# Warm-up of the tensor engine ahead of the first token tile: turnings of the identity or products in four column groups

## The reference

```python
def rms_norm(x, gain):
    xf = x.astype(jnp.float32)
    y = xf * lax.rsqrt(jnp.mean(xf * xf, axis=-1, keepdims=True) + NORM_EPS)
    return (y * gain.astype(jnp.float32)).astype(x.dtype)

for layer in range(DEPTH):                 # DEPTH = 1
    xn = rms_norm(h, norm_mix_gain[layer])
    proj = xn @ w_in[layer]
    hq, hf_fwd, hf_bwd, hi, hg, aq, ak, av, gate_a, gate_b = jnp.split(proj, IN_SPLITS, axis=-1)
    y_rec = hgrn2_mixer(hq, hf_fwd, hf_bwd, hi, hg, lb_fwd_all[layer], lb_bwd_all[layer], hg_norm_gain[layer])
    y_att = window_attention(aq, ak, av, attn_sink[layer])
    merged = jax.nn.sigmoid(gate_a) * y_rec + jax.nn.sigmoid(gate_b) * y_att
    h = h + merged @ w_out[layer]
    h = h + moe_ffn(rms_norm(h, norm_ffn_gain[layer]), ...)   # 32 experts, 4 for each token
return rms_norm(h, final_norm_gain)
```

## Time and profile before

| | us |
|---|---|
| runs of the kernel | 1752.43, 1752.76, 1756.24 |
| their median | 1752.76 |
| span of the profiled execution, first to last instruction | 1751.3 |
| TensorE busy in it | 1724.3 (98%) |
| VectorE busy | 1441.9 (82%) |
| ScalarE busy | 1140.3 (65%) |
| GpSimd busy | 518.5 (30%) |

### The profile page before, as it was taken

One profiled execution on the slowest core, in us unless ns is written; L12 is line 12 of the kernel. 1 busy time (PEld: TensorE's weight loads), 2 busy tenths in 40 slices (PEclk: granted clock), 3 DMA queues, 4 the chain that ended last, 5 costly groups with the idle time before them and its releaser, 6 DMA issues.

```text
span 1751.3 us, 26655 instructions
## 1 busy us (share of the span) xinstructions
PE 1724.3 (98%) x8893; PEld 1275.0 (73%) x8893; DVE 1441.9 (82%) x1489; ACT 1140.3 (65%) x1126; POOL 518.5 (30%) x293
## 2 busy tenths in 40 slices
PE   8999999999999999999999999999999999999997
PEld 7778777777777867677777777777777777777765
DVE  4666676567655889999998999899989998999898
ACT  4544564455454577778777777777777777777783
POOL 1102201210220144223553354334423442344340
PEclk9999999999999999999999999999999999999998
DMA  7431333133125589999999999999999999999985
GB/s 212 145 97 56 88 108 96 48 108 96 48 97 224 189 342 390 352 350 402 382 386 380 370 370 375 382 367 372 377 381 370 368 381 380 368 365 384 381 329 232
DMA packets 159188, 488.19 MB, mean 279 GB/s; under 512 B 13250, under 2 KB 83186, under 8 KB 125744
## 3 DMA queue, kind: packets, MB, share of 16 engines
q1 hardware_dynamic: 151248, 469.03, 72.6%
q0 software_dynamic: 7088, 16.52, 3.0%
q10 hardware_dynamic: 816, 2.19, 0.3%
HBM read 479.17 MB, written 24.39 MB: 288 GB/s over the span
## 4 chain that ended last, share of the span: by engine, by line
PE 92%; DVE 4%; DMA 1%; issue 1%; ACT 1%; DVEq 0%; SPq 0%; ACTq 0%
PE psum L333 27%; PE psum L335 27%; PE psum L334 27%; DVE wL L1756 2%; PE psum L714 1%; PE psum L744 1%; PE psum L1037 1%; PE psum L730 1%; PE psum L985 1%; DMA wraw<-in_w_up_gate 1%; PE psum L680 1%; PE psum L697 1%; PE psum L1001 1%; PE psum L778 0%; ACT wH L432 0%
## 5 line engine op out<-in xcount | busy, mean ns | idle before, releaser
L1756 DVE TENSOR_TENSOR wL<-wraw,wH 128x2048 fp32r<-128x2048 f32 x388 | 880.9, 2293 | 85.1 <-ACT wH L432 84.4
L432 ACT ACTIVATE wH<-wraw 128x2048 fp32r<-128x2048 f32 x388 | 744.5, 1920 | 278.6 <-PE psum L335 264.9
L333 PE MATMUL psum<-wH,xTH 128*96 128x512 f32 x1040 | 416.4, 400 | 2.0 <-DVE wL L1756 1.1
L335 PE MATMUL psum<-wH,xTL 128*96 128x512 f32 x1040 | 408.7, 393 | 0.0
L334 PE MATMUL psum<-wL,xTH 128*96 128x512 f32 x1040 | 408.1, 392 | 0.0
L2203 POOL PARTITION_BROADCAST cst<-brow x64 | 276.3, 4318 | 267.7 <-DMA xg<-x2d,ixg 218.3
L333 PEld LDWEIGHTS psum<-wH,xTH 128*96 128x96 f32 x1040 | 167.9, 161 | 74.7 <-DVE wL L1756 2.6
L335 PEld LDWEIGHTS psum<-wH,xTL 128*96 128x96 f32 x1040 | 167.8, 161 | 72.4
L334 PEld LDWEIGHTS psum<-wL,xTH 128*96 128x96 f32 x1040 | 168.0, 162 | 69.4
L333 PE MATMUL psum<-wH,aTH 128*96 128x512 f32 x496 | 197.0, 397 | 0.0
L335 PE MATMUL psum<-wH,aTL 128*96 128x512 f32 x496 | 195.4, 394 | 0.0
(11 more groups left out here) (273 smaller groups left out, 2264.2 us busy)
## 6 DMA issues: line engine op xcount, KB each, us to landing
wraw<-in_w_up_gate SPq DMA_DIRECT2D x256, 1024.0 KB, 8.2
wraw<-in_w_down SPq DMA_DIRECT2D x128, 1024.0 KB, 7.3
fraw<-in_w_in SPq DMA_DIRECT2D x68, 512.0 KB, 4.1
yd<-in_consts SPq DMA_DIRECT2D x8, 1024.0 KB, 8.0
wraw<-yd SPq DMA_DIRECT2D x3, 2048.0 KB, 9.6
wraw<-in_w_out SPq DMA_DIRECT2D x4, 1024.0 KB
xt<-in_x SPq DMA_DIRECT2D x4, 512.0 KB, 5.5
hres<-in_x SPq DMA_DIRECT2D x4, 512.0 KB, 5.1
```

The costliest lines, as they stand in the source:

```text
L333: nc.tensor.matmul(ps, lh, rh, start=start, stop=False)
L335: return nc.tensor.matmul(ps, ll, rh, start=False, stop=stop)
L432: nc.scalar.activation(wH[:, b % SPLIT, :], raw(b), ACT.Copy).then_inc(p_hi, 1)
L1756: V.tensor_tensor(wL[:, b % SPLIT, :], raw(b), wH[:, b % SPLIT, :].bitcast(F32), ALU.subtract).then_inc(p_lo, 1)
```

## The change

TensorE turns the identity four times instead of nine. It then waits until both zero fills are done and issues 42 float32 products, each with 32 columns of the identity as the stationary side and zeros as the moving one. The place of the output in PSUM (rows 0 to 31, 32 to 63, 64 to 95, 96 to 127) sets the group of 32 columns of the array that a product uses. `warm_up_groups(6, 2)` makes six rounds of four products with 512 moving columns, one in each group, and then twice nine products: two times three groups with 384 columns, and three times the fourth group with 256 columns. None of the results is used; bank 7 and bank 6 are written over by the transposes. Nothing else is changed.

```diff
+            def warm_up_groups(rounds, halves):
+
+                for r in range(rounds):
+                    for g in range(4):
+                        cols = slice(32 * g, 32 * g + 32)
+                        src = scB if g == 3 else scF
+                        nc.tensor.matmul(bank[KD - 1][cols, :], ident[:, cols], src[:, :, :].rearrange("p j c -> p (j c)"),
+                                         start=True, stop=True)
+                for r in range(halves):
+                    for n in range(3):
+                        if n < 2:
+                            for g in range(3):
+                                cols = slice(32 * g, 32 * g + 32)
+                                nc.tensor.matmul(bank[KD - 1 - n][cols, 0:3 * P], ident[:, cols],
+                                                 scF[:, n:n + 3, :].rearrange("p j c -> p (j c)") if n == 0 else
+                                                 scF[:, 0:3, :].rearrange("p j c -> p (j c)"), start=True, stop=True)
+                        nc.tensor.matmul(bank[KD - 1 - n % 2][3 * 32:4 * 32, 0:2 * P], ident[:, 3 * 32:4 * 32],
+                                         scB[:, 0:2, :].rearrange("p j c -> p (j c)"), start=True, stop=True)
+
             pe.wait_ge(id_in, 16)
-            warm_up(9)
+            warm_up(4)
+            pe.wait_ge(zeroed, 2)
+            warm_up_groups(6, 2)
             for j in range(NT):
```

## The result

The changed kernel takes 1759.93 us (median of 6 runs, 1756.36 to 1761.97), the kernel before in the same comparison 1754.03 us (6 runs, 1752.43 to 1756.24). The ratio is 1.003 with a 95% interval of 1.0019 to 1.0042: slower by 3.3 to 7.4 us. The forecast was 1758.3 us, slower, by 5.5 us. All ratios compare fast executions; one of the kernel with two rounds, at 4417 us, stands apart and is left out of its ratio.

What follows compares the result with a forecast made beforehand. TensorE, busy 98%, was taken as the bound. Products from 4.86 us put the first transpose at 13.7, L636 at 15.6, first projection at 20.2 against 14.73: 1751.3 + 5.5 = 1756.8, plus 1.46 gives 1758.3 us; 8 in 10: 1755.0 to 1767.5.

Steps and rivals of the forecast that it cites:

- The bound and the slack: TensorE bounds the kernel; warm-up may end 1.2 us later, about 8.15 us, free; later first-projection delay passes one for one.
- Turnings and clock level: Identity turnings at the start run at half clock until about 6.5 us; leaving out five saves about 2.1 us.
- The 42 products: In the warm-up, four column groups overlap wholly, 0.430 us a record, 7.74 us in all; side by side has 0.55.
- pairs-only: Rival: in the warm-up products only two of four groups overlap; +13.9 us, 1766.7 us; chance 0.12.
- threefold: Rival: the warm-up products' groups overlap only threefold, 10.3 us; +8.0 us, 1760.8 us; chance 0.08.
- no-overlap: Rival: warm-up products of 32 columns do not overlap, 31.0 us; +28.5 us, 1781.3 us; chance 0.03.
- clock's rise: During the warm-up products the clock rises near 6.5 us; 1.65 us at the lower level add 0.82 us.
- the rest: Span less the first projection's start: TensorE gets the same work past 15 us, so every later start shifts by 5.5 us.
- The 4.62 us: From L636's start to the first projection, all VectorE work in program order; said to stay 4.62 us if L636 comes later.
- The low clock through the products: Rival: clock stays low during the warm-up products, which take 15.9 us; 1767 to 1769 us; chance 0.06.
- Not slower: Rival: a 32-column product's record is shorter than the undivided array's 512-column one, so little or no loss; chance 0.16.
- its help: A front part at lower clock would cost about 3.8 us, as in the 1756.24 us run; warm projections might regain it.

Runs made afterwards that it cites:

- the kernel with two rounds: Changed kernel with two rounds of four products and none of the second kind: 1754.28 us, 0.9997 of the kernel before.
- the doubled kernel: Changed kernel with twelve rounds and four of the second kind, 84 products instead of 42: 1767.51 us, 1.0073 of the kernel before.
- the one-group kernel: Changed kernel with the same 42 products and columns, all in the first group of 32 columns: 1782.56 us, 1.0156 of the kernel before.

## Why the prediction was right

**The bound and the slack.** Right. The first projection's delay goes through: 7.6 us of time (6.6 each against its own kernel before) for 6.9 us between the first projections in the doubled kernel, 22.6 us (21.7) for 22.0 in the one-group kernel. And up to the slack's end it is free: two rounds cost nothing measurable. What the prediction did not weigh is that the start of VectorE's chain also hangs on the tiles of x: when one comes late, as in the kernel with two rounds, up to 0.7 us is lost there in a kernel with a short warm-up. Its sentence that TensorE does not wait for transfers is wrong in small: near 770 us in most profiles, and near 27 us in two, it waits, through ScalarE and VectorE, for weights. Its list of places was short as well: the kernel before also waits 0.9 us for `wL` at 738 us, among the experts, in every profile.

**Turnings and clock level.** Right: eight records in 3.01 to 5.08 us, to the hundredth those of the earlier trace rows. The fills were there.

**The 42 products.** Right, side by side. The price of a record is 0.43 us, four start within 0.02 us. The pairs-only, threefold and no-overlap rivals are out, and so is the estimate that the prediction made with the Trainium skill's figure for four row groups (TensorE: Matmul & The Clock Gate, Part 3): the trace has a factor of four, 31.0 us in one group and 7.8 in four at equal clock. The page's 3.07 is for four row groups; no run here measured those. Its 2.38, for three column groups, lies below what column groups do here, where four give a factor of four.

**The sum.** From the start of the products to the first projection, term by term in the first profile, predicted and measured:

| term | predicted | measured |
|---|---|---|
| products begin | 4.86 | 5.01 |
| products to first transpose, at the upper level | 7.74 + 0.22 + 0.05 = 8.01 | 14.69 - 5.01 - 1.85 = 7.83 |
| clock's rise, added | 0.82 | (8.70 - 5.01) / 2 = 1.85 |
| first transpose | 13.7 | 14.69 |
| first transpose to L636's place | 1.90 | 1.90 |
| from there to the first projection | 4.62 | 4.55 |
| first projection | 20.2 | 21.14 |

The term that was mis-sized is the clock's rise: it was taken from one execution, and it came between 6.5 and 8.7 us in the three profiles of the changed kernel. In the third it was at 6.49, as assumed, and the first projection at 20.04 against 20.2. The means of three profiles are 20.46 and 14.90 us, 5.6 us apart, against 5.5 forecast and a difference of medians of 5.9. That the two come so close to the forecast is in part luck: the rest, which the prediction held to be the same, varies by 1.1 us within each kernel and is 1.2 us longer in the changed one's profiles. The 4.62 us fell to 4.55 since `wsH` is long there when VectorE asks for it; it had been released 0.06 us before.

**From span to time.** The prediction took 1.46 us, the median less the span of another execution. For the profiled executions whose own time is given it is 1.9 us (1761.97 - 1760.1, 1767.29 - 1765.4). With 1.9 the forecast would have been 1758.7.

**The falls further on.** The prediction allowed up to 1.7 us for the clock near 1706 us, half of the time that it is low; the runs show 1.6. It did not foresee the falls near 606 and 630 us.

**The low clock through the products.** Out: it rose while zeros were streaming through the groups. **Not slower.** Out as well, and its help too: the front at the lower clock costs 0.6 to 0.9 us of the first projection, not 3.8. The spread between runs of the same kernel comes from the rest.

## What to carry to other kernels

Before lengthening a warm-up, find the slack of the first real instruction behind it: here 1.2 us, and each us beyond it was paid in full by a kernel that is bound by that engine to its end. Ask what the warm-up gives as well, with a kernel that has none; here real work in the same place raised the clock in time by itself. Products in four column groups are four for the price of one, which makes them cheap only per product: as a way to pass time they cost what one whole-array product of the same moving width does.

## What the runs showed of the hardware

* Four float32 products of 32 output columns and 512 moving columns each start within 0.02 us and, at the upper level of the clock, keep the 0.43 us a record of a single one; all in one group they follow one another at that pace.
* The granted clock rose during products with zeros on the moving side, and in the one-group kernel while only 32 columns of the array were in use behind the four turnings (at 6.29 us).
* In the same program the clock rose at 6.49, 6.83 and 8.70 us (in the kernel before at 6.53, 7.74 and 8.78), and it fell at other places from one execution to the next: behind the same pause of 1.51 us before the second expert in one profile and not in the others, and near 606 us with no pause over 0.4 us in the 14 us before it. One fall cost 1.6 us, in one case 1.1.
* Going to the divided array cost 0.13 us more than a 512-column product over the whole array.
